# A grouped-query layer's key and value panels taken on unnormalised rows, and a norm whose shift and rounding are one operation

## The reference, cut to what matters

```python
def rmsnorm(x, g):
    y = x * lax.rsqrt(jnp.mean(x * x, axis=-1, keepdims=True) + EPS)
    return y * g
# per layer: mod = silu(c) @ w_mod + b_mod, other values for context and latent tokens
h = rmsnorm(x, g_norm) * (1 + scale) + shift        # adaLN, before each part
x = x + gate * part(h)
# layer 2: q, k, v = split(h @ w_in); q and k are normed over 128 and rotated (RoPE), k and v also put out
o = softmax(q @ k.T / sqrt(128)) @ v;  o @ w_o
```

## Time and profile before

| | |
|---|---|
| time, median of 3 runs | 3522.38 us (3516.85 to 3526.53) |
| the profiled execution | 3524.33 us, of which the span from first to last instruction 3522.6 us |
| PE busy | 3319.7 us (94%) |
| DVE busy | 1955.6 us (56%) |
| ACT busy | 1170.8 us (33%) |
| mean granted TensorE clock | 0.972 of full speed |

### The profile page before, as it was taken

The page is one execution under the profiler, slowest core; times in us unless marked ns, Lnnn a source line. Parts: engine busy times, 40 slices in busy tenths (PEclk is TensorE's granted clock), DMA queues, the critical chain, the costliest instruction groups (busy, mean ns, idle before and its releaser), DMA issues.

```text
span 3522.6 us, 54260 instructions
## 1 busy us (share of the span) xinstructions
PE 3319.7 (94%) x20704; PEld 3051.4 (87%) x20704; DVE 1955.6 (56%) x2902; ACT 1170.8 (33%) x1850; POOL 64.8 (2%) x48
## 2 busy tenths in 40 slices
PE   7899999999989998999999888999999987999999
PEld 4776688999987775999999766899999887999999
DVE  4233356666365665685853545676663787633333
ACT  3244433111144554421112434331111586411111
POOL 1211000000000000000000000000000000000000
PEclk9999999999999998999999999999999998999999
DMA  5211125343221110253522200143432221222222
GB/s 193 57 46 37 39 81 182 126 161 126 76 69 43 43 42 17 60 202 104 186 85 66 68 18 18 54 154 127 163 123 69 75 60 44 64 78 72 77 72 77
DMA packets 443966, 304.23 MB, mean 86 GB/s; under 512 B 12483, under 2 KB 422726, under 8 KB 442822
## 3 DMA queue, kind: packets, MB, share of 16 engines
q1 hardware_dynamic: 433508, 293.75, 26.8%
q10 hardware_dynamic: 10338, 8.88, 0.8%
HBM read 298.49 MB, written 4.10 MB: 86 GB/s over the span
## 4 chain that ended last, share of the span: by engine, by line
PE 84%; ACT 6%; DVE 5%; issue 2%; DVEq 1%; ACTq 1%; DMA 1%; SPq 0%
PE psB L317 30%; PE psA L317 29%; PE psD L317 7%; PE psC L380 3%; PE psA L361 3%; PE psC L333 2%; PE psB L361 2%; PE psC L372 2%; ACT work L1553 1%; PE psD L859 1%; ACTq L1555 1%; ACT h_hi L1556 1%; PE psA L915 1%; DVE work L2587 1%; ACT work L419 1%
## 5 line engine op out<-in xcount | busy, mean ns | idle before, releaser
L1595 ACT ACTIVATE w_hi<-raw 128x1024 fp32r<-128x1024 f32 (+1 forms) x315 | 326.4, 1037 | 1118.6 <-PE psB L317 749.5
L2188 DVE TENSOR_TENSOR w_lo<-raw,w_hi 128x1024 fp32r<-128x1024 f32 (+1 forms) x315 | 375.7, 1194 | 292.8 <-ACT w_hi L1595 292.1
L317 PE MATMUL psA<-act_hi,w_hi 128*128 128x320 f32 x1600 | 373.6, 315 | 24.2 <-DVE w_lo L2188 14.9
L317 PE MATMUL psB<-act_hi,w_hi 128*128 128x320 f32 x1600 | 370.0, 312 | 9.9 <-DVE w_lo L2188 9.9
L317 PE MATMUL psA<-act_hi,w_lo 128*128 128x320 f32 x1600 | 373.1, 315 | 0.0
L317 PE MATMUL psB<-act_hi,w_lo 128*128 128x320 f32 x1600 | 371.9, 315 | 0.0
L317 PE MATMUL psA<-act_lo,w_hi 128*128 128x320 f32 x1600 | 369.2, 312 | 0.0
L317 PE MATMUL psB<-act_lo,w_hi 128*128 128x320 f32 x1600 | 368.1, 312 | 0.0
L2218 DVE SCALAR_TENSOR_TENSOR work<-work,silu_c 128x1024 f32<-128x1024 f32 x252 | 312.6, 1282 | 12.0 <-issue 0.5
L317 PEld LDWEIGHTS psA<-act_hi,w_hi 128*128 128x128 f32 x1600 | 274.0, 192 | 30.2 <-issue 20.0
L317 PEld LDWEIGHTS psB<-act_hi,w_hi 128*128 128x128 f32 x1600 | 275.5, 192 | 10.7 <-issue 10.7
(11 more groups left out here) (366 smaller groups left out, 5483.5 us busy)
## 6 DMA issues: line engine op xcount, KB each, us to landing
raw<-in_w_ffn_in SPq DMA_DIRECT2D x176, 512.0 KB, 3.8
work<-in_w_mod SPq DMA_DIRECT2D x144, 512.0 KB, 6.2
raw<-in_w_ffn_out SPq DMA_DIRECT2D x64, 512.0 KB, 4.0
raw<-in_w_ffn_out SPq DMA_DIRECT2D x32, 384.0 KB, 3.4
raw<-in_diff_w_in SPq DMA_DIRECT2D x24, 512.0 KB, 3.8
work<-in_w_mod SPq DMA_DIRECT2D x8, 1024.0 KB, 7.3
raw<-in_w_mod SPq DMA_DIRECT2D x16, 512.0 KB, 4.0
tables<-in_w_mod SPq DMA_DIRECT2D x16, 512.0 KB, 4.6
```

The costliest lines, as they stand in the source:

```text
L317: last = nc.tensor.matmul(out[:, b, 0:half], w[slot][:, kt * cols + c0:kt * cols + c0 + P], r[:, o:o + half], start=(kt == 0 and p == 0), ...
L1595: nc.scalar.activation(w_hi[s][:, 0:n], raw[s][:, 0:n], ACT.Copy).then_inc(hi_done, 1)
L2188: nc.vector.tensor_tensor(w_lo[s_][:, 0:n], raw[s_][:, 0:n], w_hi[s_][:, 0:n].bitcast(F32), ALU.subtract).then_inc(split_done, 1)
```

## The change

**All eight norms.** DVE's multiplication now applies rms and gain together, in one `scalar_tensor_tensor` for each of the two column ranges. ACT's two operations add the shift and write the rounded high part straight away; its third operation and its drain go. DVE's subtraction becomes (scaled + shift) − high, again one operation for each range. For n = 0 the early product (L2133) goes, and the loop does it behind the gains as for the others.

**Layer 2.** Four first panels in place of two: key 0, value 0, key 1, value 1, with four rescales. The sum and the rotation of key 0 stand between them. The first query panel is made into psA, in two halves with the sum of key 1 between; both ACT's and DVE's orders are rewritten by hand to match, with parts of them as steps of the norm. ACT's four cache loads move ahead of the norm.

PE's program, and what all engines share:

```diff
 TILE_UNITS = 3
+FIRST_PANELS = [0, 2, 2, 2, 4, 2, 2, 2]
 LAMBDA_INIT = 0.8 - 0.6 * math.exp(-0.3)
...
-        GKV = steps("gqa_kv", ["ssk", "rotk", "turned_v"], ["evk", "evv", "rsk", "v"], ["k", "kroped"], 0)
+        GKV = steps("gqa_kv", ["ssk", "rotk", "turned_v"], ["evk", "rsk", "evv"], ["k", "kroped"], 0)
+        GKV_V = Steps(sem("gqa_kv_v"), ["v"], 0)
...
+def rescales(n):
+    return sum(FIRST_PANELS[m] for m in range(1, n))
...
-def first_panels(n, tiles):
+def first_panels(n, tiles, then={}):
...
         pe.wait_ge(split_done, split)
-        pe.wait_ge(x_done, x_tiles[0] - 1 + k)
+        if k < 2:
+            pe.wait_ge(x_done, x_tiles[0] - 1 + k)
+        elif k < 4:
+            pe.wait_ge(rescaled, rescales(n) + k - 1)
         for kt in range(KT):
...
         last.then_inc(gemm_done, 1)
+        if k in then:
+            then[k]()
...
         ph = phases["gqa_kv"]
-        first_panels(4, [(psA, 0, ph.number(0, 0)), (psB, 1, ph.number(0, 1))])
-        for j in range(2):
-            if j == 0:
-                pe.wait_ge(rescaled, 7)
-                h_tile(psA, "gqa_kv", 1, 0, 4).then_inc(gemm_done, 1)
+        def key_sum(j):
             acts.wait(pe, "evk", j)
+            if j:
+                dves.wait(pe, "kroped", 0)
             pes.mark(sum_rows(psC, ones, [gsq], TH), "ssk")
-            if j == 0:
-                pe.wait_ge(rescaled, 8)
-                h_tile(psB, "gqa_kv", 1, 1).then_inc(gemm_done, 1)
+        def key_turn(j):
             dves.wait(pe, "k", j)
...
                      "rotk")
+        def values_turned(j):
             acts.wait(pe, "evv", j)
+            if j:
+                GKV_V.wait(pe, "v", 0)
             pe.wait_ge(gcache_in, 16 * 4)
...
             pes.mark(nc.tensor.transpose(psD[:, 1, 2 * P:3 * P], gk_t[j][:, 0:P], ident), "turned_v")
-            dves.wait(pe, "kroped", j)
-            acts.wait(pe, "v", j)
+        def first_query(part):
+            if part[0] == 0:
+                pe.wait_ge(split_done, phases["gqa"].first + 1)
+                pe.wait_ge(rescaled, rescales(4) + 3)
+            last = products(pe, psA, 0, KT, P, 0, h_hi, h_lo, 0, T, TH, part, fresh=4)
+            if part[-1] == KT - 1:
+                last.then_inc(gemm_done, 1)
+        first_panels(4, [(psum[j], j, ph.number(i, j)) for i in range(2) for j in range(2)],
+                     {1: lambda: key_sum(0), 2: lambda: key_turn(0)})
+        values_turned(0)
+        first_query(range(0, 4))
+        key_sum(1)
+        first_query(range(4, KT))
+        key_turn(1)
+        values_turned(1)
+        dves.wait(pe, "kroped", 1)
+        GKV_V.wait(pe, "v", 1)
         A, pv, out, (pes, acts, dves) = GQA
...
         h0 = Head(0, 0)
-        q_products(h0, range(KT))
         q_sum(h0)
```

ACT's program:

```diff
         for cond, (t0, t1) in enumerate(((0, NCTX), (NCTX, T))):
-            s_ = source[:, kt * T + t0:kt * T + t1]
-            nc.scalar.activation(s_, s_, ACT.Identity, bias=mod_col(layer, 3 * which, kt, cond),
-                                 scale=gains[:, cond * KT + kt:cond * KT + kt + 1])
-        act.drain()
-        nc.scalar.activation(hi[:, kt * T:(kt + 1) * T], source[:, kt * T:(kt + 1) * T],
-                             ACT.Copy).then_inc(h_hi_done, 1)
+            o = slice(kt * T + t0, kt * T + t1)
+            last = nc.scalar.activation(hi[:, o], source[:, o], ACT.Identity, bias=mod_col(layer, 3 * which, kt, cond))
+        last.then_inc(h_hi_done, 1)
         if kt in steps:
...
-    act.wait_ge(rescaled, 2 * (n - 1) + k + 1)
+    act.wait_ge(rescaled, rescales(n) + k + 1)
     for f, o in ((ACT.Square, sq), (func, out)):
...
-        norm(4, {1: lambda: high_part("gqa_kv", 1, 0), 2: first_key})
         for j in range(2):
...
             act.dma_start(gV[j][:, 5 * P:6 * P], vc[:, j, :]).then_inc(gcache_in, 16)
-        for j in range(2):
-            if j == 0:
-                acts.mark(taken(4, 1, gvt), "evv")
-                high_part("gqa_kv", 1, 1)
-            else:
-                g_panel("gqa_kv", 1, 0)
-                acts.mark(evacuate(gk_t[1][:, 0:T], gsq, psA, TH), "evk")
-                high_part("gqa", 0, 0)
-                g_panel("gqa_kv", 1, 1)
-                acts.mark(nc.scalar.activation(halves(gvt, TH), psB[:, :, 0:TH], ACT.Copy), "evv")
-                high_part("gqa", 0, 1)
+        def key_rstd(j):
             pes.wait(act, "ssk", j)
             acts.mark(rstd(act, gsq, psC, P, TH), "rsk")
+        def value(j):
+            acts.mark(taken(4, 2 * j + 1, gvt), "evv")
+        def cached(j):
             pes.wait(act, "turned_v", j)
...
             nc.scalar.activation(gk_t[j][:, T:NKEY], psD[:, 1, P:2 * P], ACT.Copy)
-            acts.mark(nc.scalar.activation(g_kout[j], psD[:, 1, 2 * P:3 * P], ACT.Copy), "v")
-            acts.wait(act, "v", j)
+            GKV_V.mark(nc.scalar.activation(g_kout[j], psD[:, 1, 2 * P:3 * P], ACT.Copy), "v")
+            GKV_V.wait(act, "v", j)
             act.dma_start(a["new_gqa_k"][0, 0][:, j, :], g_kout[j]).then_inc(outs_done, 16)
             act.dma_start(a["new_gqa_v"][0, 0][:, j, :], gV[j][:, 0:P]).then_inc(outs_done, 16)
-            dves.wait(act, "k", j)
+        norm(4, {1: lambda: high_part("gqa_kv", 1, 0), 2: first_key, 4: lambda: high_part("gqa_kv", 1, 1),
+                 5: lambda: key_rstd(0), 6: lambda: value(0)})
+        dves.wait(act, "k", 0)
+        acts.mark(taken(4, 2, gk_t[1][:, 0:T], gsq), "evk")
+        high_part("gqa", 0, 0)
+        cached(0)
+        key_rstd(1)
+        value(1)
+        high_part("gqa", 0, 1)
+        cached(1)
         outs[0] += 64
...
-        def q_taken(h):
+        def q_taken(h, ps=psD):
             act.wait_ge(gemm_done, phases["gqa"].of_head(h))
-            acts.mark(evacuate(gq_t[h.k % 2], gsq, psD, TH), "evq")
+            acts.mark(evacuate(gq_t[h.k % 2], gsq, ps, TH), "evq")
...
-        q_taken(Head(0, 0))
+        q_taken(Head(0, 0), psA)
         q_rstd(Head(0, 0))
```

DVE's program:

```diff
-dve.wait_ge(rstd_done, 1)
-for kt in range(KT):
-    nc.vector.tensor_tensor(first_scaled[:, kt * T:(kt + 1) * T], x[:, kt * T:(kt + 1) * T], first_rms,
-                            ALU.mult).then_inc(scaled_done, 1)
 pes.wait(dve, "lam")
...
     lead = 2
+    dve.wait_ge(rstd_done, n + 1)
     if n == 0:
...
         nc.vector.tensor_copy(small[:, 44:45], eps).then_inc(gains_ready, 1)
-    else:
-        dve.wait_ge(rstd_done, n + 1)
     for kt in range(KT + lead):
-        if kt < KT and n:
-            nc.vector.tensor_tensor(source[:, kt * T:(kt + 1) * T], x[:, kt * T:(kt + 1) * T], rms,
-                                    ALU.mult).then_inc(scaled_done, 1)
+        if kt < KT:
+            for cond, (t0, t1) in enumerate(((0, NCTX), (NCTX, T))):
+                o = slice(kt * T + t0, kt * T + t1)
+                last = nc.vector.scalar_tensor_tensor(source[:, o], x[:, o], gains[:, cond * KT + kt:cond * KT + kt + 1],
+                                                      (rms if n else first_rms)[:, t0:t1], ALU.mult, ALU.mult)
+            last.then_inc(scaled_done, 1)
         if kt >= lead:
-            o = (kt - lead) * T
             dve.wait_ge(h_hi_done, n * KT + kt - lead + 1)
-            nc.vector.tensor_tensor(lo[:, o:o + T], source[:, o:o + T], hi[:, o:o + T].bitcast(F32),
-                                    ALU.subtract).then_inc(h_done, 1)
+            for cond, (t0, t1) in enumerate(((0, NCTX), (NCTX, T))):
+                o = slice((kt - lead) * T + t0, (kt - lead) * T + t1)
+                last = nc.vector.scalar_tensor_tensor(lo[:, o], source[:, o],
+                                                      mod_col(n // 2, 3 * (n % 2), kt - lead, cond),
+                                                      hi[:, o].bitcast(F32), ALU.add, ALU.subtract)
+            last.then_inc(h_done, 1)
         if kt in steps:
...
-        norm(4, {1: first_key, 3: lambda: low_part("gqa_kv", 1, 0)})
-        rescale(4, 1, psB, ph.number(0, 1), gvt)
-        low_part("gqa_kv", 1, 1)
-        for j in range(2):
-            if j:
-                low_part("gqa", 0, 0)
-                low_part("gqa", 0, 1)
+        def key_normed(j):
             acts.wait(dve, "rsk", j)
             dves.mark(normed(gk_t[j][:, 0:T], vec("gqk", 1), gsq), "k")
+        def key_roped(j):
             pes.wait(dve, "rotk", j)
...
             dve.drain()
+        norm(4, {1: first_key, 3: lambda: low_part("gqa_kv", 1, 0),
+                 5: lambda: rescale(4, 1, psB, ph.number(0, 1), gvt),
+                 6: lambda: low_part("gqa_kv", 1, 1), 7: lambda: key_normed(0)})
+        rescale(4, 2, psA, ph.number(1, 0), gk_t[1][:, 0:T])
+        low_part("gqa", 0, 0)
+        key_roped(0)
+        pes.wait(dve, "turned_v", 0)
+        rescale(4, 3, psB, ph.number(1, 1), gvt)
+        key_normed(1)
+        low_part("gqa", 0, 1)
+        key_roped(1)
         A, pv, out, (pes, acts, dves) = GQA
...
         def q_normed(h):
```

(4 more changed lines are left out.)

## The result

The kernel before took 3522.1 us (median of four runs, 3516.9 to 3526.5), the changed one 3493.4 (four runs, 3490.8 to 3498.6). The ratio is 0.992, interval 0.991 to 0.994: 28.7 us less, where 22.7 were forecast.

The account below looks back on a forecast made before the run. PE carries 84% of the last-ending chain, so only its waits count; inside norms ACT sets the pace. Norms −15.3, layer 0 +10.2 and layer 2 −17.6 give −22.7: from 3522.4 to 3499.7 us, range 3490 to 3509.

Parts of the forecast that it names:

- DVE's pair, 0.93: In the norms, each DVE pair's follower starts 0.93 us after it, 1.86 per tile against 1.47, making DVE the limit.
- (b): Rival, norms: a pair's two instructions don't overlap each other, 1.17 us, costing 23 and eating all: 3522; chance 0.04.
- (a): Rival, norms: pairs are dearer; if a pair doesn't overlap its follower (1.01), sum −15: 3507; chance 0.08.
- The norms, −15.3: Norms 2, 3, 5, 6 and 7 end earlier by 3.1, 3.4, 3.4, 2.0 and 3.4 us; norm 1 gives nothing.
- Layer 0, +10.2: Late load 1 waits for the later products and holds PE; the first panel ends at 89.7, losing 10.2 us.
- (d): Rival, layer 0: the late load does not hold PE, through some missed cover: −33, 3489.5; chance 0.07.
- Layer 2, −17.6: Head of layer 2: the new order brings the first scores from 2037.0 to 2019.4, gaining 17.6 us.
- (c): Rival, layer 2: the new order locks ACT and DVE against each other and gives 9: 3508; chance 0.15.

Follow-up runs that it names:

- the triples of scalar_tensor_tensor: Changed kernel with DVE's two pairs per tile cut into three column ranges (128, 256, 256) in place of two: 3511.3 us, one run.
- that part alone: Kernel before with the new norm form in norms 1 to 7 only, layer 0 and layer 2's order as before: 3503.7 us, ratio 0.994.
- the one with the root moved: Changed kernel with the first norm's rms in a free place of the work buffer, SP not waiting for scaled_done: 3486.6 us, ratio 0.989 to the kernel before.
- the repeat: Both kernels unchanged, each profiled a second time: 3521.7 us for the kernel before, 3499.7 us for the changed one.
- the part alone: Kernel before with norm 0 alone in the new form, norms 1 to 7 and layer 2 as before: 3533.4 us, ratio 1.003.

## Why the prediction was right

**DVE's pair, 0.93: right.** The price came from a row of a like operation and held to 0.01 us, and with it the new limit: DVE without gaps, 1.85 per tile, ACT waiting. The rival that ends on the other side, (b), and (a) fall with it. The Trainium skill ("VectorE: DVE Perf Modes", section "The DRAIN you can't avoid") says that the next operation does not start until the pipe is empty; by that sentence alone rival (b) would hold, and the trace goes against it, by the pair of 1.00 us whose follower starts after 0.92. The same section of the Trainium skill adds that a next operation that is not held starts earlier, which the prediction left out and with which this trace agrees. The Trainium skill's section on the TRN2 errata (same page) gives (N+151)/0.96 ns for a float32 tensor_tensor, from which one more instruction is an estimated 0.16 us; the triples of scalar_tensor_tensor here gave 0.12 to 0.13 from start to start.

**The norms, −15.3: right in the norms' lengths, 2 to 3 us short in the stages.** With that part alone 18.8 us went by the medians, and 3.3 of these are norm 4's (its stage 317.8 for 321.1), which the forecast has inside layer 2's term: 15.5 for 15.3. That this fits so closely is in part luck, for the median has layer 0's scatter in it; the five stages of that run's profile gave 17.5. In the profiled execution of the whole change the stages of norms 2, 3 and 7 gave 3.9, 3.4 and 3.7 for 3.1, 3.4 and 3.4, norm 5's 4.6 for 3.4 and norm 6's 3.2 for 2.0; norm 1's gave nothing beyond its scatter, as said (504.5 and 503.9 after, 505.6 and 504.3 before). In norm 5's stage the excess can be seen. Windows of 5 us from the fourth panel's start, the kernel before and then the changed one:

```profile
2317.10:2322.10 5.00, 4.85 (x18) 4.88 (x19) 4.82 (x5) 0.60 (x1) 0.00 (x0) 0.50 1.10 325
2322.10:2327.10 5.00, 5.00 (x34) 5.00 (x33) 4.91 (x5) 0.53 (x2) 0.00 (x0) 0.95 0.92 337
```
```profile
2292.90:2297.90 5.00, 4.98 (x23) 5.00 (x24) 4.81 (x5) 1.06 (x1) 0.00 (x0) 0.66 1.09 329
2297.90:2302.90 5.00, 5.00 (x36) 5.00 (x35) 4.91 (x6) 1.07 (x1) 0.00 (x0) 1.00 0.90 332
```

The granted clock is 0.50 and 0.95 before, 0.66 and 1.00 after: 5 × 0.16 + 5 × 0.05 = 1.05 us of full-speed work more, and 1.2 was missing. The shortened waits stand just ahead of that panel, and the clock is back sooner. Norm 6's stage has a like excess. Windows from 60 to 200 us behind its start, the kernel before, the changed one, and the one with the root moved:

```profile
2844.60:2984.60 140.00, 113.97 (x712) 111.89 (x711) 118.75 (x164) 103.46 (x120) 0.00 (x0) 0.90 0.18 51
```
```profile
2819.20:2959.20 140.00, 114.49 (x732) 112.41 (x730) 118.52 (x165) 103.80 (x121) 0.00 (x0) 0.93 0.19 53
```
```profile
2812.30:2952.30 140.00, 115.41 (x717) 113.33 (x716) 118.06 (x163) 103.32 (x120) 0.00 (x0) 0.90 0.18 51
```

The clock is 0.93 in the changed kernel for 0.90 before. With the root moved it is 0.90 again and the stage takes 250.5 us for 248.2, though nothing in that stage differs: what norm 6 gave beyond the forecast goes with the clock and is not sure to come; how much of it the clock makes is not shown.

**Layer 0, +10.2: right, though the first profiled execution spoke against it.** Issue 74.4 forecast and 74.67 measured, landing 79.0 and 78.77, product 3.4 and 3.35, psB 89.7 and 89.19. The profiled execution then had norm 1 only 6.7 late; with the repeat it is 537.5 on the mean against 526.9, 10.6, and ten runs of the part alone say 10.5. Rival (d), no hold, falls with the 12.52 us of idle time.

**Layer 2, −17.6: right at the scores, short by what followed.** Counted from the norm's start the steps came out as put down: rotation of key 0 at 17.8 (17.9 forecast; PE waited 0.61 us before it for 1.2, since the panel ahead ended later), transposes done at 26.8 (27.0), rotation of key 1 at 34.9 (34.8), ACT free at 38.6 (38.9), first scores at 48.3 (48.4). Rival (c), a lock between the engines, falls: each step came when it was put down. The stage gained 19.1, since the heads took 1.4 us less behind it.

**The step that was mis-sized** is the sum's silence on clock behind the waits: the prediction priced it inside layer 2's query panel and in layer 0, but left every stage behind a shortened wait at its old length. Layer 2's heads (1.4), norm 5 (1.2) and norm 6 (1.2) are 3.8 of the 6.0 us by which the forecast was short. In all three the rows show a higher clock; only for norm 5 was the gain worked out from them. The rest is within the scatter of norms 1 and 2 and of layer 0. Why the clock differs in the heads and in norm 6 stays open.

## What to carry to other kernels

When operations are traded between engines, add up both engines' new load per tile and take the price from a row of the same instruction on the same ranges, start to start: here it gave the norms' lengths to 0.1 us. When work is moved behind an event, ask which loads wait for its last use of a buffer: the buffer's owner, not the arithmetic, made layer 0's 10.5 us, and a root put elsewhere gave them back. And walk a serial head (evacuate, sum, root, norm, rotate) with all engines' orders side by side: independent panels put between its steps brought the first scores 17.7 us closer to the norm's start, 10.1 of them PE's idle time and 7.6 the same work at a higher granted clock.

## What the runs showed of the hardware

A pause of PE cost more than its length: behind 3.26 us of waiting a rotation took 2.08 us for 1.02, at a granted clock of 0.50, and a panel 8.6 for 7.1, at 0.83. And the clock granted over the 200 us of heads lay anywhere from 0.94 to 0.97 in kernels whose heads are the same program, 251 to 258 us, and repeated from execution to execution. Norm 6's stage took 248.2 us at 0.93 and 250.5 at 0.90 over 140 us of the same program. A difference of some 2 to 4 us in a stage that an edit doesn't touch can thus go with the clock; what moves the clock there is not shown. Layer 0 is the opposite: its length up to norm 1 differed by 6.8 us between two executions of one and the same kernel (534.1 and 540.9), more than any other stage's.
